# Last norm by halves of its columns, no split behind the last weights, and hi and lo parts of mixing groups read out earlier

## What is computed

```python
# first block, mixing layer: 8 heads with a band of 128 keys, then 8 heads with three branches
o_b = gates[:, :, 0] * o_cmp + gates[:, :, 1] * o_sel + gates[:, :, 2] * o_win
x = x + concatenate([o_a, o_b], -1) @ w_mix_out
...
# second block, last feed-forward layer (width 2816) with a convolution over 3 tokens, and the end
u = hn @ win
y = conv_b + sum(shifted(u, tap) * conv_w[tap])
gate, val = split(y, 2)
h = h + g2[:, None, :] * ((silu(gate) * val) @ wout)
return h * rsqrt(mean(h * h, -1) + 1e-6) * final_g
```

## Time and profile before

| | |
|---|---|
| median of 3 runs | 2246.37 us (2245.47 to 2246.94) |
| the profiled execution's own time | 2246.42 us |
| its span, first to last instruction | 2244.9 us |
| PE busy | 2197.3 us (98%) |
| DVE busy | 1278.1 us (57%) |
| ACT busy | 897.6 us (40%) |
| POOL busy | 268.3 us (12%) |
| mean granted TensorE clock | 0.994 |

### The profile page before, as it was taken

How to read it: one execution, slowest core, us unless ns; L and a number is a source line. 1 busy time by engine, 2 the same in 40 slices (tenths; PEclk the granted TensorE clock), 3 DMA queues, 4 the chain that set the end, 5 groups by cost and what they waited for, 6 DMA issues and landing times.

```text
span 2244.9 us, 30960 instructions
## 1 busy us (share of the span) xinstructions
PE 2197.3 (98%) x11681; PEld 1822.1 (81%) x11681; DVE 1278.1 (57%) x2132; ACT 897.6 (40%) x1480; POOL 268.3 (12%) x445
## 2 busy tenths in 40 slices
PE   8999999999999999999999999999999999999998
PEld 6888888877788888888888888888888888888886
DVE  5764764567743363365347766456476756554654
ACT  4222223456642322225237534234264746432442
POOL 2110220044400020010027000000000530000000
PEclk9999999998999999999999999999999999999999
DMA  8954983231034284274231332332313113323322
GB/s 264 292 192 132 323 290 99 95 89 36 30 113 112 75 263 143 71 241 144 94 105 42 90 109 76 107 103 71 113 50 104 58 57 85 84 85 110 104 81 89
DMA packets 260212, 270.42 MB, mean 120 GB/s; under 512 B 9190, under 2 KB 202365, under 8 KB 260109
## 3 DMA queue, kind: packets, MB, share of 16 engines
q1 hardware_dynamic: 238381, 190.40, 28.3%
q0 software_dynamic: 21728, 78.63, 10.1%
HBM read 265.72 MB, written 12.72 MB: 124 GB/s over the span
## 4 chain that ended last, share of the span: by engine, by line
PE 88%; DVE 5%; ACT 4%; POOL 1%; issue 1%; DMA 1%; SPq 0%; DVEq 0%; ACTq 0%; POOLq 0%
PE bank L344 16%; PE bank L345 16%; PE bank L346 16%; PE bank L350 11%; PE bank L352 11%; PE bank L351 11%; PE bank L1843 2%; PE bank L1818 2%; PE bank L1796 2%; POOL probs L2003 1%; DVE w_lo L327 1%; ACT w_hi L323 1%; ACT probs L1879 1%; ACT xT_hi L772 1%; DVE probs L1945 1%
## 5 line engine op out<-in xcount | busy, mean ns | idle before, releaser
L344 PE MATMUL bank<-xT_hi,w_hi 128*128 128x512 f32 (+1 forms) x1624 | 620.4, 382 | 8.1 <-DVE xT_lo L788 3.8
L346 PE MATMUL bank<-xT_hi,w_lo 128*128 128x512 f32 (+1 forms) x1624 | 618.4, 381 | 0.0
L345 PE MATMUL bank<-xT_lo,w_hi 128*128 128x512 f32 (+1 forms) x1624 | 618.2, 381 | 0.0
L327 DVE TENSOR_TENSOR w_lo<-raw,w_hi 128x2048 fp32r<-128x2048 f32 (+2 forms) x201 | 413.2, 2056 | 326.9 <-ACT w_hi L323 325.0
L323 ACT ACTIVATE w_hi<-raw 128x2048 fp32r<-128x2048 f32 (+3 forms) x202 | 347.8, 1722 | 474.7 <-PE bank L352 418.7
L344 PEld LDWEIGHTS bank<-xT_hi,w_hi 128*128 128x128 f32 x1624 | 304.5, 188 | 70.9 <-DVE xT_lo L788 5.0
L346 PEld LDWEIGHTS bank<-xT_hi,w_lo 128*128 128x128 f32 x1624 | 304.6, 188 | 59.6
L345 PEld LDWEIGHTS bank<-xT_lo,w_hi 128*128 128x128 f32 x1624 | 304.6, 188 | 57.9
L350 PE MATMUL bank<-w_hi,hid_hi 128*128 128x512 f32 x704 | 278.0, 395 | 0.0
L351 PE MATMUL bank<-w_lo,hid_hi 128*128 128x512 f32 x704 | 277.8, 395 | 0.0
L352 PE MATMUL bank<-w_hi,hid_lo 128*128 128x512 f32 x704 | 277.7, 395 | 0.0
(11 more groups left out here) (320 smaller groups left out, 2764.2 us busy)
## 6 DMA issues: line engine op xcount, KB each, us to landing
raw<-in_ffn_w_in_dram SPq DMA_DIRECT2D x40, 1024.0 KB, 6.1
raw<-in_f_win_dram SPq DMA_DIRECT2D x40, 1024.0 KB, 6.0
mod_w<-in_mod_w_dram POOLq DMA_DIRECT2D x48, 512.0 KB, 5.4
mod_w_more<-in_mod_w_dram POOLq DMA_DIRECT2D x48, 512.0 KB, 5.9
raw<-in_ffn_w_out_dram SPq DMA_DIRECT2D x24, 768.0 KB, 4.6
raw<-in_f_wout_dram SPq DMA_DIRECT2D x24, 768.0 KB, 4.4
raw<-in_a_wqkv_dram SPq DMA_DIRECT2D x12, 1024.0 KB, 5.2
skewed_strips<-bias_strips POOLq DMA_DIRECT2D x32, 320.0 KB, 6.7
```

The lines of the kernel that those rows point to most:

```text
L327: dve.tensor_tensor(out=w_lo[:, slot, :n], in0=raw[:, slot, :n], in1=w_hi[:, slot, :n].bitcast(f32), op=ALU.subtract).then_inc(lo_done, 1)
L344: pe.matmul(o, lhsT=w[0], rhs=xs[0], start=first, stop=False)
L345: pe.matmul(o, lhsT=w[0], rhs=xs[1], start=False, stop=False)
L346: return pe.matmul(o, lhsT=w[1], rhs=xs[0], start=False, stop=last)
```

## The change

Two things.

1. The end of `ffn4`. A class `Final` replaces the last norm. The sum of squares is taken by halves of 512 columns: of the first half (columns that the panel np = 0 has finished) on ACT behind the split of the second chunk of the last panel; of the second half as soon as a block has been added to. The first half's sum, with eps, comes in as the bias of the Sqrt. DVE multiplies the first half of x by the gain ahead of the last products, ACT scales that half by the inverse (Identity), DVE scales the second half by inverse and gain. The split of the row of `final_g` on both engines is gone. The Sqrt table is loaded ahead, by a Sqrt of one column. DVE's loop over h in `ffn4` is written out. A small tile `tail` is new.
2. In round k of `att_1`, if step k-2 was a window step that ended a group, ACT takes `hi` ahead of exponentials 0 and 1, and DVE takes `lo` ahead of the inverses and the copy.

```diff
@@ Ffn.act, the last panels
                             if self.follow and h == 1 and np and q == len(OUT_KT) - 1:
                                 self.follow.end_act(act, lambda act: out_split(1, 1, len(OUT_KT) - 1), gained, second)
+                            elif self.final and h == 1 and np and q == len(OUT_KT) - 1:
+                                self.final.act(act)
                             elif np or q:
                                 out_split(h, np, q)
+                            if self.final and h == 1 and np and q == 0:
+                                self.final.first_squares_act(act)
@@ Ffn.dve
+                        if self.final and h == 1 and np:
+                            for q in range(len(OUT_KT) - 1):
+                                split_lo(dve, self.out_c(h, np, q) + 1, self.slot(q + 1), OUT_NEXT[q])
+                            self.final.end_dve(dve, product, add)
+                            continue
...
-                if first or self.follow:
+                if first or self.follow or self.final:
                     half(0, first, later)
                     half(1)
@@ PairAttention.act
+                    early = k - 2 in self.last and self.steps[k - 2].windows is not None
+                    if early:
+                        self.out_act(act, k)
                     if step and step.windows is None:
                         self.exps_act(act, k, (0, 1))
-                    if k - 2 in self.last:
+                    if k - 2 in self.last and not early:
+                        self.out_act(act, k)
@@ PairAttention.dve
+                    early = k - 2 in self.last and self.steps[k - 2].windows is not None
+                    if early:
+                        self.out_dve(dve, k)
                     large = step and step.windows is None and step.sink is None
...
-                    if k - 2 in self.last:
+                    if k - 2 in self.last and not early:
+                        self.out_dve(dve, k)
@@ the last norm
+            def squares_act(self, act, s, part):
+                act.wait_ge(x_added[s], 4 * ffn4.n + 4 + part)
+                n = (self.FIRST, self.SECOND)[part]
+                at = TOK * part + s
+                act.activation(xn_tile(s)[:, n], x[:, s, n], ACT.Square, accum_out=tail[:, at:at + 1]).then_inc(f_sq, 1)
...
+            def act(self, act):
+                self.table_act(act)
+                act.wait_ge(f_bias, 1)
+                for s in range(TOK):
+                    self.squares_act(act, s, 1)
+                    act.wait_ge(f_sq, TOK + s + 1)
+                    act.activation(tail[:, 12 + s:13 + s], tail[:, 4 + s:5 + s], ACT.Sqrt, scale=1.0 / D,
+                                   bias=tail[:, 8 + s:9 + s]).then_inc(f_sd, 1)
+                    act.wait_ge(f_gain, s + 1)
+                    act.wait_ge(f_rs, s + 1)
+                    act.activation(x[:, s, self.FIRST], x[:, s, self.FIRST], ACT.Identity, scale=tail[:, 16 + s:17 + s],
+                                   bias=zero[:, :]).then_inc(f_first, 1)
...
+            def end_dve(self, dve, product, add):
+                self.gain_dve(dve)
+                for s in range(TOK):
+                    product(s)
+                    if s:
+                        self.inverse_dve(dve, s - 1)
+                    add(s)
+                    if s:
+                        self.scale_dve(dve, s - 1)
+                self.inverse_dve(dve, TOK - 1)
+                self.scale_dve(dve, TOK - 1)
@@ SP, the stores
             for s in range(TOK):
-                sp.wait_ge(normed, s + 1)
+                sp.wait_ge(f_first, s + 1)
+                sp.wait_ge(f_second, s + 1)
                 sp.dma_start(out[0, s * P:(s + 1) * P, :], x[:, s, :]).then_inc(stored, 16)
```

More of the change, by code:

```diff
@@ L153, in program @@
         small = take("small", [P, 64])
+        tail = take("tail", [P, 20])
         neg_sink = take("neg_sink", [P, HEADS_A])
@@ L841, in __init__ @@
                 self.follow = None
+                self.final = None
                 ffns[0] += 1
@@ L1873, in act, with out_act, out_dve @@
                         act.activation(self.window_probs(k), self.window_probs(k), ACT.Exp, scale=-1.0).then_inc(self.e, 1)
+            def out_act(self, act, k):
+                act.wait_ge(self.o, self.after("o", k - 2))
+                act.activation(self.hi[:, self.last[k - 2], :], bank[7][:, :], ACT.Copy).then_inc(self.h, 1)
+            def out_dve(self, dve, k):
+                g = self.last[k - 2]
+                dve.wait_ge(self.h, self.g0 + g + 1)
+                dve.tensor_tensor(out=self.lo[:, g, :], in0=bank[7][:, :], in1=self.hi[:, g, :].bitcast(f32),
+                                  op=ALU.subtract).then_inc(self.l, 1)
             def exps_act(self, act, k, which):
@@ L2946, in program, with table_act, first_squares_act, gain_dve @@
         ffn4 = Ffn(A["f_win_2"][1], A["f_wout_2"][1], norm_ffn4, conv=1, row_gate=row_g4)
-        norm_final = Norm(ffn4.x_ready)
         final_c = chunks.take(1)
-        normed, stored = sem("normed"), sem("stored")
+        stored = sem("stored")
+        f_sq, f_bias, f_gain = sem("final_squares"), sem("final_bias"), sem("final_gain")
+        f_sd, f_rs, f_first, f_second = sem("final_sd"), sem("final_rs"), sem("final_first"), sem("final_second")
+        class Final:
+            FIRST, SECOND = slice(0, SEQ), slice(SEQ, D)
+            def squares_act(self, act, s, part):
[3 more added lines that the diff above has]
+                act.activation(xn_tile(s)[:, n], x[:, s, n], ACT.Square, accum_out=tail[:, at:at + 1]).then_inc(f_sq, 1)
+            def table_act(self, act):
+                act.activation(stat[:, 0:1], eps[:, :], ACT.Sqrt)
+            def first_squares_act(self, act):
+                for s in range(TOK):
+                    self.squares_act(act, s, 0)
+            def act(self, act):
[10 more added lines that the diff above has]
+                                   bias=zero[:, :]).then_inc(f_first, 1)
+            def gain_dve(self, dve):
+                dve.wait_ge(f_sq, TOK)
+                dve.tensor_scalar(tail[:, 8:12], tail[:, 0:4], 1.0 / D, EPS, ALU.mult, ALU.add).then_inc(f_bias, 1)
+                dve.wait_ge(raw_landed[final_c % 2], landed(final_c))
+                for s in range(TOK):
+                    dve.tensor_tensor(out=x[:, s, self.FIRST], in0=x[:, s, self.FIRST], in1=raw[:, final_c % 2, self.FIRST],
+                                      op=ALU.mult).then_inc(f_gain, 1)
+            def inverse_dve(self, dve, s):
+                dve.wait_ge(f_sd, s + 1)
+                dve.reciprocal(tail[:, 16 + s:17 + s], tail[:, 12 + s:13 + s]).then_inc(f_rs, 1)
+            def scale_dve(self, dve, s):
+                dve.wait_ge(f_rs, s + 1)
+                dve.scalar_tensor_tensor(out=x[:, s, self.SECOND], in0=x[:, s, self.SECOND], scalar=tail[:, 16 + s:17 + s],
+                                         in1=raw[:, final_c % 2, self.SECOND], op0=ALU.mult, op1=ALU.mult).then_inc(f_second, 1)
+            def end_dve(self, dve, product, add):
+                self.gain_dve(dve)
+                for s in range(TOK):
+                    product(s)
[6 more added lines that the diff above has]
+                self.scale_dve(dve, TOK - 1)
@@ L2952, in program @@
+        ffn4.final = Final()
         block = stack.enter_context(nc.Block())
@@ L3029, in _ @@
             ffn4.act(act)
-            for s in range(TOK):
-                norm_final.stats_act(act, s)
         @block.vector
@@ L3061, in _ @@
             ffn4.dve(dve)
[L3062 to L3069, removed]
         @block.tensor
```

7 lines of the change are left out of this document (removed).

## The result

| | before | with the change |
|---|---|---|
| median of 4 runs each | 2246.14 us (2245.47 to 2246.94) | **2228.26 us** (2226.82 to 2229.18) |
| the profiled execution's own time | 2246.42 us | 2229.18 us |
| its span | 2244.9 us | 2227.6 us |
| PE busy | 2197.3 us | 2180.9 us |
| DVE busy | 1278.1 us | 1275.3 us |

The ratio is 0.9918, 95% interval 0.9906 to 0.9930: 17.9 us less, where 4.3 were forecast.

What follows compares the result with a forecast made beforehand. PE was taken as the bound (88% of the chain), so time goes only where PE stands still or behind its last matmul. 2246.42 - 3.4 (end) - 0.9 (mixing groups) = 2242.1 us, range 2240.5 to 2243.7.

Steps and rivals of the forecast that it cites:

- The written-out loop ... PE keeps its pace there, zero: DVE's loop in `ffn4`: writing it out was to gain or cost nothing, since PE keeps its pace.
- what PE sets and the change leaves alone: Program end: the last product's start, 2234.86 us, was taken as set by PE and untouched by the change there.
- the chain's 88% PE: Chain that ended last, by engine: 88% PE, so time goes only where PE stands still or behind its last matmul.
- The end, -3.4 us: Behind the last product: the last scaling ends at 2238.47 instead of 2241.84, 3.4 us less, bounds 2.5 and 3.7.
- The groups, -0.9 us: Three mixing group ends: 0.31 us less each, 0.9 in all; bounds 3.0 less and 0.5 more.
- The split between the two waits: Mixing group end: first values only 0.20 us earlier of a 0.80 wait; of the second set's hidden 0.21, 0.10 stays.
- The hidden wait of 0.21: Second set of 20 value matmuls takes 1.52 us, the first 1.31; lost to an ACT copy, 0.10 was to stay.
- the clock: Rival: TensorE's clock falls to 0.80 in the three mixing groups, up to 11.5 us more, 2253.6 us; chance 0.02.
- the norms kept PE's pace: Rival at the end: the last norm slips 0.2 us in each of three blocks, 2.8 instead of 3.4, 2242.7; chance 0.09.
- the five: Rivals: groups gain more (0.14) or nothing (0.13), last norm slips (0.09), clock falls (0.02), DMA sets end (no own chance).
- more in the groups: Rival: PE gets back the whole 0.80 or whole hidden wait, 0.5 to 1.0 us a group, 2240.0 to 2241.5; chance 0.14.

Runs made afterwards that it cites:

- B: PE alone, 48 matmuls with high stationary and low moving operand: 227.0 ns with no tile out of phase, 232.7 with low stationary 128 bytes out.
- C: PE alone, 48 matmuls with low stationary and high moving operand: 226.0 ns with no tile out of phase, 233.9 with low stationary 128 bytes out.

## Why the prediction was wrong

- **"The written-out loop ... PE keeps its pace there, zero", and "what PE sets and the change leaves alone"**: the step that failed lies behind both. I costed the instructions and the waits of the change, and never the one line of the diff that allocates. The tile `tail` appears in no term of the sum. It was put at nothing without a reason. It moved the tiles behind it by 128 bytes, and that alone gives 13.7 of the 17.9 us. The loop itself does cost zero.
- The profile before had a trace of it that I did not follow. Two groups of one form and with next to no idle time, L344 with 390 ns and L350 with 395, differ in nothing but which tiles they read. That 5 ns had no explanation, and the chain's 88% PE were taken as fixed.
- **The end, -3.4 us**: right. 3.3 by the trace of the change, and 3.3 by the medians of the kernel with this part alone. Square 0.61 for 0.63 taken, Identity 0.81 for 0.82; DVE's scaling of 512 columns with a scalar of its own took 0.75, not 0.69, and is still not the last. The last instruction ends 3.73 behind the product's start, 3.61 forecast: the final Square started 0.17 behind the add's end rather than 0.11 (the Identity ahead of it ran until 2222.55), and the last Identity 0.26 behind its inverse rather than 0.19. The Trainium skill, page "ScalarE: Activation LUTs", section "What ACT_TABLE_LOAD costs", gave 0.61 and 0.80: for this Square the rows agree better with it than with my neighbour's 0.63.
- **The groups, -0.9 us**: right in size, 0.30 a period for 0.31, though by the traces; the runs alone can't tell it from nothing. The split between the two waits was wrong. The first set of values starts 0.36 earlier and not 0.20: `lo` began 0.08 sooner behind the reads ahead of it, the copy 0.07 behind the inverse instead of 0.09, and the values followed it by 0.10 instead of 0.15. The hidden wait of 0.21 in the second set stays whole, where 0.11 of it was to go. The two errors cancel, because ACT's copies came 0.30 earlier, for 0.31 forecast, and the second set gains just that.
- With no address moved the change takes 2241.26 us, against 2242.1 forecast, inside the range; its interval, 3.4 to 7.9 us less, takes in the two terms (3.3 + 0.9 = 4.2). With the shift on top, 4.2 + 13.7 = 17.9, which is what was measured; that it fits to the tenth is chance. By the medians of the same chip the parts add up to 5.7 + 13.7 = 19.4, the change run again gave 18.5, and each of these has an interval of some 2 us or more to either side.
- **Rivals**: the clock did not fall in the groups (1.00 from 539.7 to 616.6 us, 0.995 over the whole); the norms kept PE's pace. None of the five had a mechanism by which PE itself would run faster, so the low end of the range had nothing below "more in the groups".

## What to carry to other kernels

Treat every allocation as a part of a change: write down which tiles it moves and by how much, and compare the addresses of the two operands of the long matmul streams. In this kernel, 512 column fp32r matmuls whose operands lie a multiple of 256 bytes apart start every 227 to 228 ns, others every 229 to 234, and an unused tile was worth more than the two clever edits together. Other types were not run, and with 256 columns being in phase was the slower case, so measure before carrying the distance over. When two groups of the same form and with no idle time differ by a per cent or two, ask which tiles they read before calling PE's time fixed.

## What was not expected of the hardware

- The pace of back-to-back matmuls depends on the distance between the stationary and the moving operand within a partition, modulo 256 bytes: 226.7 to 227.7 ns in phase, 229.0 to 229.1 at 192, 232.1 to 234.2 elsewhere, with no other engine at work. It holds for 512 columns; for 256 columns being in phase is 1.3 to 2.2 ns slower (120.0 ns).
- The Trainium skill, page "TensorE: Matmul & The Clock Gate", section "Step-by-step: what each phase is for", says that TensorE reads the two operands through two independent ports of SBUF, so that loading the next stationary tile takes nothing from the running matmul, and that matmuls follow each other at the length of the stream, about 216 ns for 512 columns. The page gives no figure for fp32r, and none of the fp32r streams here is faster than 226.7 ns. The 5.7 ns between 232.4 and 226.7 depend on how the two operands lie to each other, which two reads without any bearing on each other would not explain. But loading beside a running matmul is not shown to be what costs them: with the low stationary operand alone out of phase, B and C are both slow, and only B has its load beside it. Which reads meet, and what they share, the runs don't show.
